# Paced background steps, a block pipeline for the first latents, four score banks in the first attention

## The reference

```python
z = rmsnorm(h) @ w_in            # u | c_q | c_kv | k_rope | gate_a | gate_b
a = pool_mixer(u) @ pool_w * s   # trailing means over 2, 4, 8, 16 positions
q = rmsnorm(c_q) @ w_uq          # 16 heads of 64 + 32 rotated
k, v = rmsnorm(c_kv) @ w_ukv     # 64 + 64 a head, rotated k_rope shared
b = causal_softmax(q k) v
h = h + (sigmoid(gate_a) * (a @ w_pa) + sigmoid(gate_b) * (b @ w_pb)) @ w_o
h = h + (silu(rmsnorm(h) @ w_gate) * (rmsnorm(h) @ w_up)) @ w_down
```

## Time and profile before

| what | us |
|---|---|
| median of 3 runs | 4899.67 (4890.97 to 5296.59) |
| profiled execution | 4910.89 |
| span of its slowest core (core 2) | 4909.4 |
| spans of all cores | 4866.2 to 4909.4 |
| TensorE busy | 4467.1 (91%) |
| weight loads on TensorE | 2934.8 (60%) |
| VectorE busy | 2177.9 (44%) |
| ScalarE busy | 2289.3 (47%) |
| mean granted clock of cores 0 to 7 | 0.963 to 0.974 of full |

### The profile page before, as it was taken

One profiled execution on the slowest core, in us unless ns is written; L12 is line 12 of the kernel. 1 busy time (PEld: TensorE's weight loads), 2 busy tenths in 40 slices (PEclk: granted clock), 3 DMA queues, 4 the chain that ended last, 5 costly groups with the idle time before them and its releaser, 6 DMA issues.

```text
span 4909.4 us, 108476 instructions; the slowest of 8 cores (4866.2 to 4909.4 us)
## 1 busy us (share of the span) xinstructions
PE 4467.1 (91%) x38386; PEld 2934.8 (60%) x38888; DVE 2177.9 (44%) x4547; ACT 2289.3 (47%) x4989; POOL 206.0 (4%) x392
## 2 busy tenths in 40 slices
PE   3688899999999979999999989999999999999998
PEld 1344566666656656656666656666666656656555
DVE  3666544344354354344444444434444434344342
ACT  2577754454455455455455455445445452121221
POOL 0000000000000000000000000000000000000000
PEclk8899999999999999999999999999999999999987
DMA  5210344654555455555555555455454465676754
GB/s 133 66 44 31 71 92 86 126 114 96 105 126 91 90 131 99 100 126 102 98 127 97 97 129 102 82 125 98 92 123 98 81 135 115 121 154 115 146 93 85
DMA packets 153547, 508.47 MB, mean 104 GB/s; under 512 B 16448, under 2 KB 94528, under 8 KB 127296
## 3 DMA queue, kind: packets, MB, share of 16 engines
q0 software_dynamic: 56640, 348.51, 40.5%
q1 hardware_dynamic: 96384, 152.99, 9.8%
HBM read 782.44 MB, written 67.50 MB: 173 GB/s over the span
## 4 chain that ended last, share of the span: by engine, by line
PE 80%; DVE 8%; ACT 5%; issue 4%; DMA 2%; DVEq 0%; ACTq 0%; POOL 0%; SPq 0%; POOLq 0%
PE ps L343 80%; ACT sb_pt L351 2%; DVE sb_nx L357 2%; DMA sb_wb<-wst 1%; DVE sb_zb L361 1%; DVE sb_h L357 1%; ACT L351 1%; ACT sb_sg L351 1%; DMA sb_smalls<-smalls 1%; ACT sb_rstd L351 1%; DVE sb_qh L378 1%; DVE sb_hn L357 1%; DVE sb_qh L354 0%; ACT sb_nx L351 0%; DVE sb_eab L354 0%
## 5 line engine op out<-in xcount | busy, mean ns | idle before, releaser
L343 PE MATMUL ps<-sb_hn,sb_wb 128*128 128x344 bf16 x12288 | 2027.1, 314 | 100.6 <-DVE sb_sg L357 28.6
L351 ACT ACTIVATE sb_pt<-ps 128x512 bf16<-128x512 f32 (+4 forms) x2624 | 1299.3, 531 | 868.7 <-PE ps L343 858.2
L343 PEld LDWEIGHTS ps<-sb_hn,sb_wb 128*128 128x128 bf16 x12288 | 1190.2, 99 | 728.7 <-issue 124.5
L343 PE MATMUL ps<-sb_act,sb_wb 128*128 128x344 bf16 x6528 | 1041.1, 311 | 18.1 <-DVE sb_h L357 12.1
L343 PEld LDWEIGHTS ps<-sb_act,sb_wb 128*128 128x128 bf16 x6528 | 632.2, 98 | 345.2 <-issue 25.8
L343 PEld LDWEIGHTS ps<-sb_vh,sb_pt 128*128 128x128 bf16 x9792 | 582.8, 97 | 381.2 <-issue 189.9
L343 PE MATMUL ps<-sb_vh,sb_pt 128*128 128x65 bf16 x9792 | 732.0, 194 | 86.2 <-ACT sb_pt L351 68.3
L343 PE MATMUL ps<-sb_qh,sb_kh 128*128 128x16 bf16 (+4 forms) x3263 | 776.9, 288 | 0.0
L357 DVE SCALAR_TENSOR_TENSOR sb_sg<-sb_sg,ps 128x344 f32<-128x344 f32 x528 | 270.8, 513 | 737.3 <-ACT sb_sg L351 699.4
L351 ACT ACTIVATE sb_sg<-ps 128x344 f32<-128x344 f32 x576 | 263.5, 457 | 618.9 <-PE ps L343 609.6
L357 DVE SCALAR_TENSOR_TENSOR sb_h<-ps,sb_h 128x344 f32<-128x344 f32 x384 | 197.7, 516 | 677.3 <-PE ps L343 676.6
(11 more groups left out here) (65 smaller groups left out, 2526.4 us busy)
## 6 DMA issues: line engine op xcount, KB each, us to landing
sb_wb<-wst POOLq DMA_DIRECT2D x176, 1024.0 KB, 8.8
sb_wb<-wst POOLq DMA_DIRECT2D x96, 896.0 KB, 8.1
sb_wb<-wst POOLq DMA_DIRECT2D x96, 704.0 KB, 6.9
sb_h<-xT SPq DMA_DIRECT2D x20, 1376.0 KB, 10.6
nS<-sb_nx SPq DMA_DIRECT2D x24, 688.0 KB, 4.7
sb_hn<-nS SPq DMA_DIRECT2D x24, 688.0 KB, 5.0
sb_bx<-bS SPq DMA_DIRECT2D x24, 688.0 KB, 8.4
hS<-sb_h SPq DMA_DIRECT2D x12, 1376.0 KB, 9.7
```

Source lines behind the costliest of these rows:

```text
L343: return P.op("pe", lambda e: e.matmul(out, lhsT, rhs, start=start, stop=stop), reads, writes, inc)
L351: return P.op("act", lambda e: e.activation(out=out, in_=in_, func=func, **kw), reads, writes)
```

## The change

Background steps now carry a cost and are spent by credit: `bgrun(c)` adds `rate` times the unit's cost (0.65, and 1.0 in the last stage) and emits steps while credit is left. A float in the queue is a delay, counted down by units' costs (3000 ahead of a norm's multiplies, 2500 ahead of those of the latents, which go to the queue's front). A string is a mark; `upto(mark)` emits all up to it, and stands where a result is needed, mostly in place of `flush`.

Stage A becomes `first_alone`: the small constants are loaded ahead of h, h's first block comes in four pieces, and the sums of block i+1 and squares of block i+2 are emitted around the latents of block i, with copies of z on ScalarE. In the first attention the scores get a fourth bank (7), LA is 4, and `dps` has banks 5 and 6; later attentions are as before. Loads of WA are emitted one head later. Squares of z are taken from PSUM, or one unit late where VectorE copies. The pool's sum has one buffer for a span. Turns have a new order, the pooled product of a span after a layer-1 span moves into the next span's first gates, the meta copy moves into the gates, and `gate_out` comes ahead of the second norm. The last wo units and first FFN units weigh 1.5 in `weave`. Tracking of the act buffer is finer (cells at the edges of what is used).

```diff
+        x[1]()
+        c = x[2] if len(x) > 2 else x[0]
+        if c:
+            bgrun(c)
...
-        wsum = [zb_t[:, i * SPAN:(i + 1) * SPAN] for i in range(2)]
+        wsum = [zb_t[:, 0:SPAN], eab[0][:, :]]
...
+        deep = [True]
+
         def dps():
-            b = 5 + dring[0] % 3
+            b = 5 + dring[0] % (2 if deep[0] else 3)
             dring[0] += 1
...
+            b = (0, 1, 2, 7)[sring[0] % (4 if deep[0] else 3)]
...
+        credit = [0.0]
+        rate = [0.65]
+
+        def bgpop():
+            x = bg.popleft()
+            if x.__class__ is tuple:
+                x[1]()
+                return x[0]
+            return 0.0
+
+        def bgrun(c):
+
+            if bg and bg[0].__class__ is float:
+                bg[0] -= c
+                if bg[0] > 0.0:
+                    return
+                bg.popleft()
+                credit[0] = 0.0
+            credit[0] += rate[0] * c
+            while bg and bg[0].__class__ is not float and credit[0] > 0.0:
+                credit[0] -= bgpop()
+            if not bg:
+                credit[0] = 0.0
+
+        def upto(mark):
+            if mark in bg:
+                while bg[0] != mark:
+                    bgpop()
+                bgpop()
 
         def flush():
-            bgrun(len(bg))
+            while bg:
+                bgpop()
 
         DMA("sp", meta[:], metaT, P.new_dma_sem(), (), [cst["meta"]])
...
-                if hd % 4 == 3:
-                    out.append((0.0, lambda: next_wa(hd // 4)))
+                if hd % 4 == 0 and hd:
+                    out.append((0.0, lambda: next_wa(hd // 4 - 1)))
...
-            LA = 3
+            LA = 4 if (s, l) == (0, 0) else 3
...
+                if j == len(tiles) - per // 2:
+                    units.append((0.0, lambda: next_wa(NH // 4 - 1)))
...
+            return [3000.0] + [(520.0, lambda c=c: STT(dst[:, b, c, :], h[:, b, c, :], sm(l, gcol + c), rstd[b][:], ALU.mult,
+                                                       ALU.mult, [hB[b][c], rstdB[b], cst["smalls"]], [dstB[b][c]]))
+                               for c in range(KC)]
...
+            def soon(steps, mark):
+                bg.extendleft(reversed([2500.0] + steps + [mark]))
...
+                if j == 0:
+                    for m in "qk":
+                        upto("%s%d_%d" % (m, s, i - 1))
...
-                    ACT(sqq[j][:], zb[:, j, :], AF.Square, [zbB[j]], [sqqB[j]])
+                    if ev == "act":
+                        ACT(sqq[j][:], PS[x][:, :BLK], AF.Square, [PSB[x]], [sqqB[j]])
+                if ev == "dve" and j in (1, 2):
+                    sq_late(j - 1)
...
+                soon([(590.0, lambda j=j: STT(cqn[s][:, j, t0:t0 + BLK], zb[:, j, :], sm(l, SM_QG + j), rq[:], ALU.mult, ALU.mult,
+                                              [zbB[j], rqB, cst["smalls"]], [cqnB[s][i]])) for j in range(2)], "q%d_%d" % (s, i))
...
+                soon([(590.0, lambda: STT(ckvn[s][:, t0:t0 + BLK], zb[:, 2, :], sm(l, SM_KVG), rk[:], ALU.mult, ALU.mult,
+                                          [zbB[2], rkB, cst["smalls"]], [ckvB[s][i]])),
+                      (2100.0, rope_k)], "k%d_%d" % (s, i))
...
-                units += [("gap", 2500.0), (0.0, flush)]
+                units += [("gap", 8000.0), (0.0, lambda i=i: upto("h%d" % i))]
...
-                r = g % 2
+                r = 0 if l == DEPTH - 1 and (s, sp) != (0, 0) else 1
...
+                upto("p%d_%d" % (k, g))
...
+                    out.append((c * (1.5 if b else 1.0), lambda b=b, m=m: job(b, m), c))
...
+                gate_out()
                 bg.extend(norm_fin(1, l, SM_GFFN, hn, hnB))
-                gate_out()
-
-            out += [(mm_ns(2 * KC, BLK), late)] + first[1:8] + [(0.0, flush)] + first[8:]
+
+            out += [(c * 1.5, f, c) for c, f in [(mm_ns(2 * KC, BLK), late)] + first[1:8]] + [(0.0, flush)] + first[8:]
             for i in range(2, FC // 2):
...
+                return u[:3] + nrm[:1] + u[3:5] + nrm[1:] + u[5:]
+            a = a_units(k + 1)
+
+            def tile():
+                wl[0] = wtile((l + 1) * NT_LAYER, TW)
+
+            def ready(b):
+                return [(0.0, lambda: upto("n%d_%d" % (k, b)))]
+
             u0, t0 = lat_units(s, l + 1, 2 * sp, wl, "act")
             u1, t1 = lat_units(s, l + 1, 2 * sp + 1, wl, "act")
-            return out + u0[:2] + a[:2] + u0[2:] + u1[:1] + t0 + u1[1:] + a[2:] + t1
+            return (u[:1] + [(0.0, tile)] + u[1:3] + nrm[:1] + u[3:5] + nrm[1:] + ready(0) + u0 + t0 + u[5:] + ready(1) + u1 + a[:2] + t1
+                    + a[2:] + [(0.0, flush)])
 
...
+                if j == 4 and spans[k][1:] == (0, 0):
+                    out.append((0.0, meta_in))
+                g = gates(k, j)
+                if j == 0 and k and spans[k - 1][1] == DEPTH - 1:
+                    g = g[:5] + a_units(k) + g[5:]
+                out += g
...
+        def first_alone():
+            wl = {}
+            consts("smalls")
+            load_first()
+            wl[0] = wtile(0, TW)
+            load_h(0, 0, 1)
+            consts("rope", "invc")
+            constants()
+
+            def squares(i):
+                for m in range(KC):
+                    square(i % 2, m)
+
+            def sums(i):
+                bg.extend(norm_fin(i % 2, 0, SM_GMIX, nx, nxB))
+
+            def normed(i):
                 flush()
+                store_hn(0, 0, i)
+                if i + 2 < NB:
+                    load_h(0, 0, i + 2)
+
+            squares(0)
+            sums(0)
+            normed(0)
+            squares(1)
+            for i in range(NB):
+                if i + 1 < NB:
+                    sums(i + 1)
+                u, t = lat_units(0, 0, i, wl, "act")
+                held = list(bg)
+                bg.clear()
+                for c, f in u[:3] + u[4:]:
+                    f()
+                bg.extend(held)
+                if i + 1 < NB:
+                    normed(i + 1)
+                for c, f in u[3:4] + t:
+                    f()
+                flush()
+                if i + 2 < NB:
+                    squares(i + 2)
+
...
+        first_alone()
         pre = [(0.0, lambda: (load_span(load_hn, 0), load_span(load_h, 0)))] + u_units(0) + [(0.0, flush)] + a_units(0)
-        weave(attention(0, 0, "dve"), first_latents(1) + pre, bg, bgrun)
-        weave(attention(1, 0, "act"), tokens(0), bg, bgrun, 1.03)
-        weave(attention(0, 1, "act"), tokens(1), bg, bgrun, 1.03)
-        weave(attention(1, 1, "act"), tokens(2), bg, bgrun, 1.03)
-        weave([], tokens(3), bg, bgrun)
+        weave(attention(0, 0, "dve"), first_latents(1) + pre, bgrun)
+        deep[0] = False
+        weave(attention(1, 0, "act"), tokens(0), bgrun, 1.03)
+        weave(attention(0, 1, "act"), tokens(1), bgrun, 1.03)
+        weave(attention(1, 1, "act"), tokens(2), bgrun, 1.03)
+        rate[0] = 1.0
+        weave([], tokens(3), bgrun)
```

119 lines of the change are left out of this document (56 added, 63 removed).

## The result

The changed kernel took **4821.3 us** (median of three runs), the kernel before beside it 4891.0 and 4899.7 in the two runs compared: a ratio of **0.9848, interval 0.982 to 0.9877**. That is about 74 us less where 145 were forecast, and less than the 2% (98 us) that the prediction took for its line. By it the kernel before stands at 4872.5 to 4875.0 on the five other chips used, the changed one at 4815.2 and 4815.4.

What follows compares the result with a forecast made beforehand. Stage A was taken as a dependency chain, B near TensorE and ScalarE limits, C and D as TensorE-bound with holes. Terms -30 - 35 - 21 - 7 - 26 - 15 - 11 = -145 on 4910.9 gave 4766, median 4755, range 4690 to 4815.

Steps and rivals of the forecast that it cites:

- Rival (b): Whole kernel: bank swap and forced steps cancel Part 2 and Part 5, giving 4816 us; chance 0.22.
- two signs of being wrong: Stage B not shorter, or waits on nx and hn in stage C passing 60 us.
- Part 1: Stage A, first sequence's latents: blocks overlap as a pipeline, -30 us, bounds -17 (cycle 17.4) and -34.
- Part 3: Attention's weight loads: issued one head later, they stop holding up the next weight tiles; -21 us (-15 to -25).
- meta: Turn to sequence 1: moving the meta copy into the gates removes a 6.50 us wait; -7 us, once.
- Part 4: FFN entries: tanh first, less idle; -10 us over three alone, -16 over nine beside attention, -26 in all, bounds 0 and -56.
- Part 2: Stage B, first attention: fourth score bank, look-ahead 4, late squares and pacing; -35 us, between 0 and about -75.
- Part 5: Turns between spans, new order: layer-0 turns -15 us (bounds +10 and -40), turns after layer-1 spans -11.
- Rival (c): 48 norms reach forced points unfinished, TensorE waits 4.6 us each: +221, whole kernel slower at 5028 us; chance 0.05.
- Layer-1 turns: Turns after layer-1 spans: VectorE's chain decides; -1 us each in D, -3 each beside attention, -11 in all.
- The base: Sum taken from the profiled execution's 4910.9 us; the median of the runs lies 11.2 lower.
- Rival (d): Stage D: denser work holds the clock at 0.81, +143 us, whole kernel 4898; chance 0.05.

Runs made afterwards that it cites:

- e3: Kernel before the change with one edit: the load of the attention's weights issued one head later; 4866.2 us.
- e4: Kernel before the change with one edit: at the FFN entry the first gate's tanh and product come ahead of the second norm; 4874.6 us, ratio 0.9978.
- e17: e13 with the written delays halved (1500 and 1250 ns); 4780.0 us, cores' median 4767.8.
- e16: e13 with pacing rate 1.0 in place of 1.3; cores' median 4732.8 us.
- e6: Changed kernel with the old unit order only in the turns after a layer-1 span; 4822.0 us.
- e13: Changed kernel with pacing rate 1.3 and, in the first attention, three score banks, three for other products, look-ahead 3; 4739.4 us, ratio 0.969.
- e15: Changed kernel at rate 0.65 with the written delays ahead of paced steps taken out; 4789.8 us.

## Why the prediction was wrong

The sign was right and half of the size was lost. Rival (b), "the bank swap and the forced steps cancel parts 2 and 5", gave 4816 and is what happened; it had a chance of 0.22. Of the prediction's two signs of being wrong one came: B is not shorter. The other, waits on nx and hn in C above 60 us, did not: 39.5 on nx and none on hn. The pooled products, with 36.0, it did not have on the list.

- **Part 1, stage A, -30: held.** -30.5 by the first attention matmul (121.46 against 151.94; "near 120" was forecast), -26.7 by the first score matmul (140.22 against 166.88), -26.3 by the mark. The head lost 6.8 more than computed, since block 1's load was late, and cycles of 14 and at last 10.65 for 14.5 made that up. What is missing lies behind: the latents' tail into the attention got 4 us longer, and the banks and the look-ahead have 2.4 of A. The bound for a cycle of 17.4 should have been -15, not -17.
- **Part 3, loads -21, meta -7: held.** e3 alone gave -17; the 6.50 us wait is gone.
- **Part 4, entries -26: too large.** The gate's order alone gave 11 to 13 (e4). In D it gave 9.6 of the 10 forecast; beside attention it gave 5 where 16 were forecast, and TensorE waited more for q copies. The pacing's share isn't isolated; e4 and e17 show that the delays keep VectorE off roots that aren't there (60.2 against 20.0 us).
- **Part 2, stage B, -35: wrong, and the step that failed is the choice between its bounds.** "The nearest row is ScalarE's wait for zb, 26.7, which goes for certain, plus some of the rest." It went, and B came out 3.4 longer on core 6 and 2.1 by the means. Two things were wrong. A wait of ScalarE was booked as time of the stage, but the stage is bound by TensorE and ScalarE in turn, and ScalarE's idle time went from this wait to waits for scores (71.1 to 113.6). And the two banks cost more than the four with their look-ahead gained: 9 us at rate 0.65, 19 at 1.3. With three banks and rate 1.3 B is 460.7 by the mean of the cores, 12 below the kernel before: even then a third of the forecast.
- **Part 5, layer-0 turns, -15: wrong in kind.** The prediction had the numbers in hand, 28 us of steps, divided by 0.65, plus 16 of delays, against 44 of TensorE work, and drew from them that "much of it is therefore forced out at the points where it is needed, as now". Not as now. Before, steps were let out by count, early, and the price was 40.2 us of waits on q copies in C; here most stand late, and each forced point then has TensorE wait for a burst: 39.5 us for nx and 36.0 for pooled products in C, of which none was there before by these names. The same sum, worked on, gives the rate that is needed: 28 us in 44 - 16 = 28 us of work, 1.0, and 1.0 did as well as 1.3 (e16). At 1.3 C is 94 us shorter than before the change by the mean of the cores (3311.5 for 3405.8), against about 68 forecast. Rival (c) named this mechanism, priced it at 4.6 us a norm over 48 norms, and dismissed it; it came at 3.3 us over 12.
- **Layer-1 turns, -11: about nothing**, as e6 shows: 6 won beside attention (9 forecast), 7 lost in D (2 to be won). The chain in D was right in its steps, but VectorE stood 3.88 us for the pooled copies ahead of block 1's multiplies, and TensorE behind them 7.64 and 3.62. With the old order (e6) D is 15 shorter than before the change, of which e4's edit alone has 9.6.
- **The base.** The sum was taken from an execution whose slowest core had 0.81 of its clock at the end; D took 856.7 us on it and 826.6 to 830.0 on the six cores other than 2 and 3. Of the 74 us that the ratio gives, the cores' medians show 58 (4873.0 to 4815.4) and the slowest core of a die 64 (medians 4883.2 to 4818.9); the other 10 lie in the two runs of the kernel before, 4891.0 and 4899.7, and not in the change.

Counted together: A 24, loads 17, meta 7 (its wait, not a run of its own), entries 11 make 59, and the cores' medians differ by 58 (4873.0 against 4815.4). Parts 2 and 5, forecast at 61, came to nothing. That the sum comes out so near is in part luck, as each term is off by a few us. Set right by the rate and by the banks with their look-ahead, the change is worth 142 to 151 us (e13: 4739.4 against 4890.3 beside it, cores 4730.9 against 4872.5).

## What to carry to other kernels

A paced queue needs its budget worked out where it is fullest: steps divided by the rate, plus the delays, must fit in the work that is there before the forced point, or the pacing turns into the burst that it was to prevent, now on the critical path. In these runs it did not pay to go far above that rate either (2.6 was 20 us worse than 1.3). Price an order of units only with the pacing that it will run with: the same order cost 25 us at one rate and won 20 at another. A bank that one ring wins another loses; read what the ring that gives the bank waits for now. And don't book an engine's idle time as time of the stage when another engine takes turns with it at being the bound.

## What was unexpected

- Half of the delay cost 37 us at rate 1.3 (e17), while no delay at 0.65 won 32 (e15). What one setting is worth hangs on the other.
- Waits for weight tiles differed between cores of one execution: 18.7 us on core 2 and 17.5 on core 0, but 8.8 on core 6 of the kernel before, with the same program. The cores of that kernel fall into two groups, at about 4865 and 4880. The late load is the cause: in two traces with it, of the kernel before and of e4, the four cores with 15.7 to 18.7 us of it are those with the longer C (3408 to 3415 for 3397 to 3400, and 3404 to 3412 for 3392 to 3396), though they are cores 0, 2, 4, 7 in the one and 0, 3, 5, 7 in the other. In e3, whose only edit is that load, C is 3387 to 3393 on all eight. Which four it hits, and why, stays open.
- Fewer holes did not bring a lower clock: of the cores that "cores" counts, those of e13 were granted 0.979 to 0.983 over the whole run and those of the kernel before beside them 0.970 to 0.974. Rival (d) found nothing for it here.
